# Cached latents and position keys requested in blocks and turned by VectorE in 32x32 blocks

## The reference

```python
def _sample_attention(qn, qp, kn_new, kp_new, v_new, cache_ckv, cache_kpe, layer, page_table, w_ukv, g_kn):
    def step(carry, phys):
        c_blk = cache_ckv[layer, phys]              # (8, 128, 256) latents of one page per sequence
        kp_blk = cache_kpe[layer, phys]             # (8, 128, 32)  position keys
        kn_blk, v_blk = _decompress(c_blk, w_ukv, g_kn)   # RMS norm of each key head needs c_blk @ w_ukv
        return _merge(carry, _attn_partial(qn, qp, kn_blk, kp_blk, v_blk, None)), None
    carry, _ = lax.scan(step, init, page_table.T)
    ...
```

## Time and profile before

| what | value |
|---|---|
| median of 3 runs | 1370.22 us (1369.78 to 1373.98) |
| time of the profiled execution | 1373.91 us |
| its span in the trace | 1372.0 us |
| TensorE busy | 1301.0 us (95%) |
| VectorE, ScalarE, GpSimd busy | 707.8, 459.9, 150.8 us |
| granted TensorE clock, mean | 0.973 |
| instructions | 26075 |

### The profile page before, as it was taken

One profiled execution on the slowest core, in us unless ns is written; L12 is line 12 of the kernel. 1 busy time (PEld: TensorE's weight loads), 2 busy tenths in 40 slices (PEclk: granted clock), 3 DMA queues, 4 the chain that ended last, 5 costly groups with the idle time before them and its releaser, 6 DMA issues. The chain is left out here.

```text
span 1372.0 us, 26075 instructions
## 1 busy us (share of the span) xinstructions
PE 1301.0 (95%) x9543; PEld 750.1 (55%) x9543; DVE 707.8 (52%) x1749; ACT 459.9 (34%) x1108; POOL 150.8 (11%) x182
## 2 busy tenths in 40 slices
PE   5999999699999999999989999999999999989898
PEld 3545677556666666555445445666544444445343
DVE  3001436644665656555737876667666666520321
ACT  3001343233343433332434433434344444310220
POOL 0000314400020201114402230000000000000000
PEclk9999999789999999999999999999999999998999
DMA  5422121101111111131141113221334221101000
GB/s 206 155 74 54 32 62 32 52 19 37 37 37 37 37 37 37 37 71 36 40 129 41 40 39 113 97 90 43 86 112 116 68 69 53 49 0 35 16 16 35
DMA packets 82995, 81.49 MB, mean 59 GB/s; under 512 B 18946, under 2 KB 76611, under 8 KB 82868
## 3 DMA queue, kind: packets, MB, share of 16 engines
q1 hardware_dynamic: 80452, 73.87, 18.1%
q10 hardware_dynamic: 2416, 5.96, 1.2%
HBM read 75.72 MB, written 4.07 MB: 58 GB/s over the span
## 5 line engine op out<-in xcount | busy, mean ns | idle before, releaser
L500 PE MATMUL PS<-wk,c_T 128*128 128x512 f32 x1024 | 500.8, 612 | 0.0
L627 DVE TENSOR_REDUCE ssq<-sq__69 128x8 f32<-128x512 f32 x256 | 175.4, 685 | 221.1 <-ACT sq__69 L554 218.7
L500 PEld LDWEIGHTS PS<-wk,c_T 128*128 128x128 f32 x1024 | 176.3, 192 | 163.0 <-issue 145.7
L554 ACT ACTIVATE sq__69<-PS 128x512 f32<-128x512 f32 x256 | 152.8, 597 | 320.5 <-PE PS L500 320.2
L455 PE MATMUL PS<-cst,c_ring 128*128 128x128 f32 x512 | 83.0, 287 | 24.7 <-DVE c_ring L663 10.1
L1470 PE MATMUL PS<-xnT,w_ring 128*128 128x276 f32 x416 | 104.7, 409 | 0.0
L455 PEld LDWEIGHTS PS<-cst,c_ring 128*128 128x128 f32 x512 | 60.4, 147 | 69.7 <-issue 45.0
L1304 PE MATMUL PS<-w_ring,xnT 128*128 128x424 f32 x256 | 95.3, 530 | 2.1 <-DMA w_ring<-in_w_in 2.1
L1470 PEld LDWEIGHTS PS<-xnT,w_ring 128*128 128x128 f32 x416 | 79.9, 195 | 21.9 <-issue 4.1
L1304 PEld LDWEIGHTS PS<-w_ring,xnT 128*128 128x128 f32 x256 | 48.5, 193 | 46.8 <-issue 44.3
L2655 PE MATMUL PS<-w_g,nT 128*128 128x512 f32 x128 | 56.0, 594 | 0.0
(11 more groups left out here) (534 smaller groups left out, 1873.3 us busy)
## 6 DMA issues: line engine op xcount, KB each, us to landing
c_ring<-in_cache_ckv SPq DMA_DIRECT2D x256, 128.0 KB, 2.8
w_ring<-in_w_in SPq DMA_DIRECT2D x4, 1696.0 KB, 14.4
w_ring<-in_w_in SPq DMA_DIRECT2D x9, 512.0 KB, 5.0
r_ring<-in_cache_kpe SPq DMA_DIRECT2D x256, 16.0 KB, 1.8
w_o<-in_w_out SPq DMA_DIRECT2D x8, 512.0 KB, 3.7
w_g<-in_w_ple_gate SPq DMA_DIRECT2D x8, 512.0 KB, 3.6
xn<-in_x_prompt SPq DMA_DIRECT2D x4, 512.0 KB, 7.0
w_ring<-in_w_in SPq DMA_DIRECT2D x2, 1024.0 KB, 5.8
```

What stands on the lines that cost most here:

```text
L500: mm = pe.matmul(PS[:, NORM[v % 2], :], c_T[:, u % 2, k, t * P:(t + 1) * P], wk[:, k], start=(k == 0), stop=(k == 1))
L554: nc.scalar.activation(sq_[:, v % 2, :], PS[:, NORM[v % 2], :], ACT.Square).then_inc(no_sb, 1)
L627: dve.tensor_reduce(ssq[:, u % 2, t * H:(t + 1) * H], sq_[:, v % 2, :].rearrange("p (h c) -> p h c", h=H), AX.X, ALU.add).then_inc(red_sb, 1)
```

## The change

**The walk over the cache.** Every latent is now fetched twice: as before into `c_ring` for `values` (line 425 of the new file), and in blocks of 32 positions by 64 values into a new buffer `c_blocks` (line 433, 16 transfers of 32 x 4 x 64 values a step), laid so that VectorE can turn it in 32x32 blocks straight into `c_T` (lines 616 and 617). The position keys come in 16 transfers of 32 x 32 values (line 440) in place of four, and are turned by VectorE too (line 623). TensorE's transposes and the copies of their results out of PSUM are gone; the copy of the dot products goes from VectorE to ScalarE. `c_ring` has two places in place of four, `c_blocks` two. All transfers are issued by SyncE. A request for blocks waits for the turn of the step two before it, a request for latents for `values` two steps before.

```diff
-RING = 4
+RING = 2
+R_RING = 4
...
+        def latent_blocks(u, page):
+            for x in range(GT):
+                rows_x = io["cache_ckv"][bass.ds(page[x], 1)].rearrange("o (p t) c -> (o p) t c", t=GT)
+                for g in range(4):
+                    nc.sync.dma_start(c_blocks[32 * g:32 * g + 32, u % RING, :, x, :],
+                                      rows_x[:, :, g * (KVL // 4):(g + 1) * (KVL // 4)]).then_inc(b_in[u % RING], 16)
+
+        def rope_pages(u, page):
+            for x in range(GT):
+                rows_x = io["cache_kpe"][bass.ds(page[x], 1)].rearrange("o (p t) c -> (o p) t c", t=GT)
+                for t in range(GT):
+                    nc.sync.dma_start(r_ring[32 * t:32 * t + 32, u % R_RING, 32 * x:32 * x + 32], rows_x[:, t, :]
+                                      ).then_inc(r_in[u % R_RING], 16)
+
         def pages_sp():
             sp = nc.sync
+            for u in range(blocks_ahead):
+                rope_pages(u, page_numbers(u))
+            for u in range(pages_ahead, RING):
+                latent_pages(u, page_numbers(u))
+            sp.wait_ge(ct_sb, 1)
+            page = page_numbers(RING)
+            latent_blocks(RING, page)
+            rope_pages(RING, page)
+            yield
             for u in range(NSTEP):
-                page = page_numbers(u)
                 if u >= RING:
+                    page = page_numbers(u)
                     sp.wait_ge(vv_ps, u - RING + 1)
                     sp.sem_inc(slot_taken, 1)
-                if u >= ahead_pages:
                     latent_pages(u, page)
...
+                v = u + RING + 1
+                if v < NSTEP:
+                    page = page_numbers(v)
+                    sp.wait_ge(ct_sb, v - RING + 1)
+                    sp.sem_inc(slot_taken, 1)
+                    latent_blocks(v, page)
+                    if v >= R_RING:
+                        sp.wait_ge(tn_sb, v - R_RING + 1)
+                    rope_pages(v, page)
                 yield
...
             def turned_c(u):
-                dve.wait_ge(k0_ps, u + 1)
-                dve.tensor_copy(c_T[:, u % 2, 0, :], PS[:, TURN, :]).then_inc(k0_sb, 1)
...
+                dve.wait_ge(b_in[u % RING], 16 * GT * 4 * (u // RING + 1))
+                if u >= 2:
+                    dve.wait_ge(rp_ps, u - 1)
+                    dve.wait_ge(no_ps, (u - 1) * GT)
+                parts_c = c_blocks[:, u % RING].rearrange("p t x (k c) -> p k (t x) c", k=2)
+                dve.transpose(c_T[:, u % 2, 0, :].rearrange("p (b q) -> p b q", q=32), parts_c[:, 0])
+                dve.transpose(c_T[:, u % 2, 1, :].rearrange("p (b q) -> p b q", q=32), parts_c[:, 1]).then_inc(ct_sb, 1)
...
-        on_sp = Stream(pages_sp(), lambda slot: min(NSTEP, max(RING, (slot - 2) // GT + RING - 1)))
+        on_sp = Stream(pages_sp(), lambda slot: min(NSTEP + 1, slot // GT + 1))
```

```diff
                     for k in range(KD):
                         mm = pe.matmul(PS[:, u % 4, 0:w], xnT[:, k, i * P:(i + 1) * P], w_ring[:, c % 2, k, 0:w],
                                        start=(k == 0), stop=(k == KD - 1))
+                        if c == 0 and k == KD // 2 - 1:
+                            turn(i + 1)
...
-                    pe.matmul(bank(u % 2)[:, 0:w], qT[:, h, i * P:(i + 1) * P], k_T[:, h, 0:w], start=True, stop=False)
-                    pe.matmul(bank(u % 2)[:, w - P:w], ident, con("causal"), start=False, stop=True).then_inc(sc_ps, 1)
+                    pe.matmul(bank(u % 2)[:, 0:w], qT[:, h, i * P:(i + 1) * P], k_T[:, h, 0:w], start=True, stop=True
+                              ).then_inc(sc_ps, 1)
...
                     dve.wait_ge(sc_ps, u + 1)
+                    V(dve.tensor_tensor(bank(u % 2)[:, w - P:w], bank(u % 2)[:, w - P:w], con("causal"), ALU.add))
```

More of the change, by code:

```diff
@@ L258, in build @@
         pages_at = place.at = w_ring_at
+        c_blocks = place("c_blocks", [P, RING, GT, GT, KVL // 4])
         c_ring = place("c_ring", [P, RING, GT, KVL + 1])
@@ L443, in pages_pe @@
             pe = nc.tensor
[L445 to L464, removed]
             def dots(u):
                 pe.wait_ge(tn_sb, u + 1)
+                if u >= 1:
+                    pe.wait_ge(rp_sb, u)
                 pe.matmul(PS[:, TURN, P:2 * P], q_rope[:, u // STEPS].rearrange("p x q -> p (x q)"), r_T[:],
@@ L502, in norms @@
                 mm.then_inc(no_ps, 1)
[L504 to L506 removed]
+            yield
+            yield
             for u, t in slots:
[L508 to L522, removed]
+                if t == 0 and u >= 2:
+                    turn_weights(u - 2)
+                if t == 1 and u >= 2:
+                    values(u - 2)
+                if t == 2 and u >= 1:
+                    turn_scale(u - 1)
                 if t == 3:
@@ new lines, in chunk_pe @@
+                mm.then_inc(l_ps, 1)
+                for h in range(H):
+                    for ck in HALVES:
+                        mm = pe.matmul(eight(2, ck)[:, at_head(h), :], gram[ck, at_head(h), 2, :],
+                                       vn[ck, i, h * HN:(h + 1) * HN], start=True, stop=True)
+                mm.then_inc(w_ps, 1)
+                on_pe.go(2)
+                pe.wait_ge(low_sb, 3 * i + 1)
+                products(0, gram[:, :, 0], low[:, 0])
+                products(1, low[:, 0], gram[:, :, 0]).then_inc(y2_ps, 1)
@@ new lines, in chunk_pe @@
+                on_pe.go(1)
+                pe.wait_ge(u5_sb, i + 1)
+                pe.wait_ge(low_sb, 3 * i + 3)
+                turns(3, ua)
+                products(0, low[:, 2], ua).then_inc(t5_ps, 1)
+                on_pe.go(1)
+                pe.wait_ge(t5_sb, i + 1)
+                products(1, pa[:, 0], pa[:, 1]).then_inc(u6_ps, 1)
+                on_pe.go(1)
+                pe.wait_ge(u6_sb, i + 1)
+                for o in range(H):
+                    for ck in HALVES:
+                        mm = pe.matmul(bank(2 + o // 4)[ck, (o % 4) * P:(o % 4 + 1) * P], ub[ck, o, :], aw[ck, o, :, :],
+                                       start=True, stop=True)
```

1663 lines of the change are left out of this document (833 added, 830 removed).

## The result

The changed kernel takes 2282.03 us (median of 4 runs, 2278.80 to 2284.35) against 1372.10 us (median of 4, 1369.78 to 1374.93) of the kernel before on the same chip: a ratio of 1.663, 95% interval 1.659 to 1.667. The forecast of 2330 us was 48 us too high, the range held it. The profiled execution took 2284.35 us with a span of 2282.5 us.

The account below looks back on a forecast made before the run. SyncE's serial issue was taken as the bound: its queue, 1895 us from 238.7, ends at 2134 us, last norms at 2154, output stage 181 more, less small corrections: 2330 us, range 2000 to 2480 us.

Parts of the forecast that it names:

- The mechanism: Cache walk: SyncE issues 36 transfers and eight loads serially, so every step goes at its pace, 28.05 us.
- The terms of one step: SyncE's issue per step: latents 3.05, blocks 12.2, keys 8.0, page numbers 4.8, together 28.05 us.
- the rival in which blocks are as cheap as keys: On SyncE, blocks issue as cheaply as keys: 266 us less, 2065 us; chance 0.13.
- The whole queue: SyncE from its first page load at 238.7 us to the last keys at 2134 us: sum 1895 us.
- the long transfers: SyncE's transfers that take longer than the median: 51 us for keys and 25 us for others, 76 us.
- The turns: VectorE's new transposes, taken at 0.68 us for latents and 0.3 us for keys; priced at nothing under SyncE.
- The estimate of 1.24 us for 128x512: VectorE's transpose of 128x512 as four 128x128 blocks of 311 ns in bf16; leaves the sum as it is.
- The clock: Sign that the forecast is right: TensorE's clock partly at 0.5.
- the clock rival: Waiting TensorE drops to 1.2 GHz: up to 2 us on 41 interleaved steps, 2330 to 2410 us; chance 0.12.
- One sign: Sign that the forecast is right: TensorE busy under 60%.
- The transfers: DMA engines are not the limit: a step's 512 large and 2560 small packets take at most 6.7 us.
- The faster rival: SyncE's issue is not the bound, TensorE stays it and gives back its transposes: about 1240 us; chance 0.04.

Follow-up runs that it names:

- e1: The changed kernel with blocks and keys requested for the first two steps only and turned again in later steps: 1335.88 us.
- e2: The changed kernel with the 16 key transfers of a step, with their own four page loads, issued by ScalarE in place of SyncE: 1933.70 us.
- e10: The changed kernel with each step's page numbers loaded once and kept in registers for both kinds of request: 2123.25 us.
- e7: The kernel before with each of a step's four key transfers cut into four, 16 in all, the same bytes to the same places: 1487.65 us.
- e6: As e1, with the two turns of the latents on VectorE moved to the second and fourth quarters of a step: 1316.42 us.
- e9: The kernel before with all of the change but the cache walk, wk's rows in the old walk's order: 1352.46 us, ratio 0.984.
- e4: The changed kernel with blocks and keys each in one transfer a page, 12 transfers a step: 1630.57 us.

## Why the prediction was right

**The mechanism held.** The prediction's first claim was that SyncE's issuing sets the pace of the steps. Issue made free gives 1336 us (e1), issue shared between two queues 1934 (e2), eight page loads cut to four 2123 (e10), and the old kernel with nothing but more issue slows as soon as its slack is gone (e7).

**The terms of one step.** Predicted: 3.05 of latents, 12.2 of blocks, 8.0 of keys, 4.8 of loads, 28.05 us together. Measured from 1974.33 to 2002.41: 28.08 us. The value in doubt was the blocks', taken from the latents because they have the same number of pieces, and not from the keys because they have as few bytes: 564 ns against the latents' 572. That choice was worth the 265 us to the rival in which blocks are as cheap as keys.

**The whole queue.** SyncE's stretch from its first page load to the last keys is 1850 us (235.3 to 2085.1) where the sum had 1895, and these 45 us are nearly the whole error. Counted on SyncE from the start of each instruction to the start of the next, the predicted value with its share of the additions in brackets: blocks 788 us (798), keys 544 (563), latents 192 (191), page loads 289 (301), stores and weights 26 (20), waits and barriers 11 (22). The term mis-sized most is that of the long transfers: 76 us were added to the counted ones, and 47 came. It carried the old kernel's mean of 2.15 us for four keys over to 16, and now a group of 16 has a mean of 8.31 us where the quiet one has 7.91. What runs long is mostly the first of a group, here the first key transfer and the other 15 of the step at 1992.02 us:

```profile
L440 SPq DMA_DIRECT2D r_ring<-in_cache_kpe x1: 447/447/447, 1992.0 to 1992.0; - x1
L440 SPq DMA_DIRECT2D r_ring<-in_cache_kpe x15: 315/316/316, 1992.7 to 1999.6; - x15
```

The first has a median of 0.445 us over all groups of 16, and had 0.446 in the groups of four before. Key transfers of over 0.41 us were 73 of 256 before, 61 of them the first of a group, and are 79 of 1024 now, 60 of them the first. What the first ones take above 0.316 us stayed at 8 us in all, and that of the others grew from 10 to 17, where the sum let both grow by four. Behind the keys the last norms follow after 16.7 us (20 predicted), and the output stage takes 181 us as before.

**VectorE.** The turns were taken at 0.68 and 0.3 us and took 0.71, 0.67 and 0.30. The estimate of 1.24 us for 128x512, worked out from the Trainium skill (VectorE: DVE Perf Modes, The three transpose paths), was nearly twice too high: that page's figure is for another type and size. It bore no weight under SyncE, but e1 shows what it would have meant: with issue free, 1.3 us of turns at the wrong place in VectorE's order already cost TensorE half a microsecond a step.

**The clock.** The sign came as told, and without a price. It was granted at 0.67 on the mean in the last stage. Behind 13 us of idling it was 0.50, the level of 1.2 GHz (2025.0 to 2028.6 us, four matmuls in 3.62 us), and 1.00, the level of 2.4 GHz, a little later (2029.5 to 2031.4 us, four in 1.98). The steps there stayed at 28.1 to 29.0 us, the sum of SyncE's work, so the slower TensorE cost nothing. The steps of the interleaved stages stayed at 28 to 30.3 us with three of 33.5 and one of 32.5, each with stores, weights or a wait of SyncE's own in it, so the clock rival did not occur. One sign was missed narrowly: TensorE is busy 61%, where under 60% was told.

**The transfers.** Predicted not to be the limit, and the 18.4% of queue 1 and the landing after 2.1 us agree; e2, with the same packets in 348 us less, and e10, with the same queue in 159 us less, show it.

**The faster rival.** It had 0.04 and was refuted with the mechanism. But it was priced wrong too: with the issue of blocks and keys gone the change gives 1336 us, not 1240. Its steps: 22.6 us for the rest of the change, where the prediction had some 35; 0.97 us a step for the transposes instead of 1.5, because busy times of overlapping groups were added (34 us in 64 steps); a new bound on VectorE (19 us between e1 and e6); and one wait of 17.7 us in e1 for the first `r_T`. Together they are some 83 of the 96 us. This rival would have won by the Trainium skill's rule (DMA: Bandwidth & Descriptors, Issuing engines are not separate DMA queues) that initiating is "usually small relative to the DMA itself". The runs disagree for this kernel: the issue of a block is 0.77 us with its register work against 2.1 us to landing, and as 36 issues stand in line while landings overlap, the sum of issues counts and the single ratio says nothing.

**What stays open.** Whether the dearer issue of a merged transfer comes from its number of pieces, from its further dimension or from the number of partitions was not separated. What holds a transfer that is issued behind one of 512 pieces, so that it takes 1.6 us in place of 0.65 or 0.54, was not tested either, nor why the first of a group of keys takes longer than the rest. Which of the small edits give e9 its 22.6 us was not tried apart.

## What to carry to other kernels

Before a transfer is split, write down one step of the queue that issues it: every transfer at its own issue time, the register loads and the gaps included, against the step's period. Here it was 8 transfers with 5.8 us of slack on the mean and 2.0 in the last stage (37.2 us over 19 waits), and 36 could not fit. Take the slack of each stage by itself: 4 more transfers a step used up the last stage's. Slack makes the first extra ones nearly free (0.02 us each) and the later ones not (0.21 us each on the mean, 0.5 in the last stage), so a test with a few says nothing of many. And a gain on the bound engine is worth what the stretch gets shorter, not the busy time of the group that goes; e6 gave two thirds of it, and only after the next engine's order was mended.

## What the runs showed of the hardware that was not expected

- Among transfers with an address from a register, the issue time on SyncE went with the number of pieces and not with the bytes: medians of 0.316 us for 32 pieces of 128 or of 512 bytes, and of 0.56 to 0.57 us for 128 pieces of 128, 256 or 1024 bytes. One of 512 pieces of 256 bytes took 0.65 us as the first of its group and 1.6 us right behind others of its kind (e4). A weight of 128x1024 values, without a register, took 0.42 us. The four loads of page numbers cost 2.4 to 2.5 us on top, nearly a tenth of the changed kernel's step for each set.
- The first key transfer of a group took 0.445 us and the ones behind it 0.316, in groups of four and of 16 alike.
- ScalarE computes nothing while it issues: 16 transfers of 32 pieces and four loads took 10.4 us out of it.
- VectorE turns 128x512 in 32x32 blocks in 0.67 to 0.71 us and 128x128 in 0.30 us, no more than a copy of the same size out of PSUM took (0.68 us).
